# A two-layer decoder step: first weights and parameters fetched a layer ahead, semaphores cleared in two parts, page transposes spread

## What is computed

```
h  = rmsnorm(x);  x += 0.5 * rmsnorm((silu(h @ wg) * (h @ wu)) @ wd)      # f1, width 2816
h  = rmsnorm(x);  proj = h @ w_in                                          # A, B, C, gates
   A: RWKV-7 time mixing;  B: dilated window attention (8 K/V heads)
   C: latent attention: scores = q_lat . ckv + q_rope . krope over 2048 paged rows and the own ones
m  = sum_b gate_b * (y_b @ w_branch_b);  x += rmsnorm(m @ w_out)
h  = rmsnorm(x);  x += 0.5 * rmsnorm((silu(h @ wg) * (h @ wu)) @ wd)      # f2
```

## Time and profile before

| | us |
|---|---|
| median of 3 runs (3042.34 to 3046.57) | 3046.08 |
| the profiled execution | 3031.76 |
| its span | 3030.2 |
| TensorE busy | 2807.8 (93%) |
| VectorE busy | 959.1 (32%) |
| ScalarE busy | 520.8 (17%) |
| mean granted TensorE clock | 0.976 |
| first matmul of layer 0 | at 35.11 |
| first matmul of layer 1 | at 1543.98 |

### The profile page before, as it was taken

How to read it: one execution, slowest core, us unless ns; L and a number is a source line. 1 busy time by engine, 2 the same in 40 slices (tenths; PEclk the granted TensorE clock), 3 DMA queues, 4 the chain that set the end, 5 groups by cost and what they waited for, 6 DMA issues and landing times.

```text
span 3030.2 us, 44033 instructions
## 1 busy us (share of the span) xinstructions
PE 2807.8 (93%) x18588; PEld 1892.8 (62%) x18588; DVE 959.1 (32%) x2503; ACT 520.8 (17%) x1094; POOL 62.9 (2%) x84
## 2 busy tenths in 40 slices
PE   5999999999999888999869999899998998899996
PEld 3776656656656555676647676566566665567764
DVE  1220344345524342221112204444455244422211
ACT  1000121123411221100010001211334112120000
POOL 0000000000000100000000000000000001000000
PEclk9999999999999999999979999999999999999998
DMA  5434599853931423343243345998548314243431
GB/s 174 136 94 116 177 335 324 306 205 140 358 148 56 156 91 129 101 131 96 58 147 111 110 121 182 337 323 306 178 192 338 115 57 163 83 139 111 125 101 56
DMA packets 257499, 502.03 MB, mean 166 GB/s; under 512 B 10192, under 2 KB 196944, under 8 KB 242064
## 3 DMA queue, kind: packets, MB, share of 16 engines
q1 hardware_dynamic: 248848, 327.69, 32.8%
q0 software_dynamic: 8448, 171.45, 15.4%
HBM read 491.95 MB, written 140.85 MB: 209 GB/s over the span
## 4 chain that ended last, share of the span: by engine, by line
PE 89%; DVE 4%; ACT 3%; DMA 2%; issue 1%; SPq 1%; POOL 0%; DVEq 0%; ACTq 0%; POOLq 0%
PE ps L605 82%; PE ps L608 7%; DMA ring<-in_f_wu_dram 1%; DVE ring L2102 1%; DMA ring<-in_cache_mla_ckv_dram,pidx 0%; ACT big L1461 0%; ACT reg L1461 0%; DMA big<-in_cache_swa_k_dram 0%; DVE ring L2064 0%; DMA ptab<-in_page_table_dram 0%; DVE reg L1598 0%; ACT ring L1520 0%; DVE x L1609 0%; DVE ring L1992 0%; SPq L544 0%
## 5 line engine op out<-in xcount | busy, mean ns | idle before, releaser
L605 PE MATMUL ps<-h,ring 128*128 128x320 f32 (+1 forms) x3840 | 1078.2, 438 | 84.1 <-DMA ring<-in_f_wu_dram 74.0
L605 PEld LDWEIGHTS ps<-h,ring 128*128 128x128 f32 (+1 forms) x3840 | 725.4, 191 | 391.6 <-issue 99.9
L605 PE MATMUL ps<-big,ring 128*128 128x320 f32 (+3 forms) x2624 | 508.2, 371 | 22.1 <-DVE big L1621 8.1
L605 PEld LDWEIGHTS ps<-big,ring 128*128 128x128 f32 (+2 forms) x2624 | 351.4, 170 | 191.4 <-issue 41.0
L605 PE MATMUL ps<-ring,h 128*128 128x512 f32 (+3 forms) x896 | 246.2, 469 | 0.0
L1616 DVE TENSOR_TENSOR big<-ps,reg 128x320 f32<-128x320 f32 x88 | 43.2, 491 | 598.5 <-PE ps L605 598.5
L608 PE MATMUL ps<-cst,big 128*128 128x128 f32 x944 | 140.2, 284 | 26.2 <-ACT big L1461 7.3
L605 PEld LDWEIGHTS ps<-ring,h 128*128 128x128 f32 (+1 forms) x896 | 103.2, 163 | 80.6 <-issue 65.0
L1334 ACT ACTIVATE reg<-big 128x320 f32<-128x320 f32 x88 | 41.5, 471 | 647.7 <-DVE big L1616 647.7
L605 PE MATMUL ps<-reg 128*16 128x8 f32 (+13 forms) x1864 | 142.1, 276 | 2.3 <-DVE sml L1871 1.2
L1591 DVE TENSOR_TENSOR h<-h 128x320 f32<-128x320 f32 x36 | 17.7, 492 | 387.6 <-ACT h L1325 387.6
(11 more groups left out here) (255 smaller groups left out, 2196.9 us busy)
## 6 DMA issues: line engine op xcount, KB each, us to landing
out_o_swa_k_s_dram<-in_cache_swa_k_dram POOLq DMA_DIRECT2D x16, 4080.0 KB, 15.2
out_o_swa_v_s_dram<-in_cache_swa_v_dram POOLq DMA_DIRECT2D x16, 4080.0 KB, 16.4
ring<-in_w_in_dram SPq DMA_DIRECT2D x30, 2048.0 KB, 11.2
ring<-in_f_wg_dram SPq DMA_DIRECT2D x44, 1024.0 KB, 5.4
ring<-in_f_wu_dram SPq DMA_DIRECT2D x44, 1024.0 KB, 7.9
ring<-in_f_wd_dram SPq DMA_DIRECT2D x32, 1408.0 KB, 7.0
big<-in_cache_swa_k_dram SPq DMA_DIRECT2D x32, 1024.0 KB, 8.3
ring<-in_cache_swa_v_dram SPq DMA_DIRECT2D x32, 1024.0 KB, 6.9
```

The costliest lines, as they stand in the source:

```text
L605: return pe.matmul(out, lhsT, rhs, start=first, stop=last, skip_group_check=True)
```

## The change

- At the start the order of loads is x, parameters, first weight unit, constants, second and third unit. The engines wait for x alone; the constants (`s_const`) and the parameters (`s_next`) have semaphores of their own. The page table is loaded from GpSimd's queue.
- Parameters are loaded to a second buffer `parn`, for the next layer while this one is in f1, and copied to `par` by VectorE at the layer's start; the scaling of the first norm reads `parn`.
- The first three `gu` units of f1 (`HEAD`) are loaded for the next layer as the last three `d` units of f2 are used; the slots are shifted by one so that they fit (`turn` starts at 1). In the last layer they are loaded too and not used.
- 125 semaphores are cleared in f2 between the units d 0 and d 1, 18 at the layer's end. Some step semaphores are merged.
- x is stored to `yT` at the end of each layer, in two halves, and that store is waited for ahead of the last clearing.
- In each FFN the loop over k takes two column tiles instead of three, and the sum of squares stands behind k = 5, not 4.
- In `ml_sample` each group of four transposes stands alone between pieces of other work; the scores are issued in three pieces and the values in two, the values of b-2 now in the first half of batch b. VectorE's and ScalarE's lists follow.
- The product of branch c is split: the prompt's 256 columns are done in and behind the last steps of `ml_sample` (`prompt_branch`, with banks from `TAIL_BANK` = (4, 5, 0, 1, 2, 3, 7, 6)), the samples' 64 columns in `mix`.

```diff
-    slot, last, before, turn = [], {}, [], 0
+    slot, last, before, turn = [], {}, [], 1
     for i, (name, _) in enumerate(units):
...
-            at = (2, 0, 1, 0, 1, 0, 1)[name[1]]
+            at = (0, 1, 0, 1, 0, 1, 0)[name[1]]
         elif name[0] == "pg":
-            at = (0, 1, 0, 1, 1, 0)[name[1]]
+            at = (1, 0, 0, 1, 1, 0)[name[1]]
         elif name[0] in ("br", "wo"):
-            at = {"a": 0, "b": 0, "c": 0, 0: 1, 1: 2}[name[1]]
+            at = {"a": 1, "b": 0, "c": 0, 0: 1, 1: 2}[name[1]]
...
-        per_layer = [s_dve, s_par, s_sml, s_out, s_state, s_wkv, s_shin, s_shout] + s_vw + s_kw + s_slot + list(S.values())
+        to_the_end = ("ffn_a", "ffn_gu", "ffn_sg", "ffn_t", "nsum", "norm_sums", "normed", "roots", "logs", "squared", "down_d",
+                      "down_y", "x")
+        cleared_early = [s_par, s_sml, s_out, s_state, s_wkv, s_shin, s_shout] + s_vw + s_kw + [S[n] for n in STEPS if n not in to_the_end]
+        cleared_last = [s_dve] + s_slot + [S[n] for n in to_the_end] + [s_out]
...
+            def first_weights(l, u):
+                i = uidx[heads[u]]
+                at = slot_of[i] * SLOT
+                for src, k, n in units[i][1]:
+                    sp.dma_start(ring[:, at:at + k * n].rearrange("p (k n) -> p k n", k=k), src(l)).then_inc(s_head[u], 16)
+                    at += k * n
+
             sp.dma_start(x, io["xT"]).then_inc(s_once, 16)
-            for i in range(8):
-                sp.dma_start(ptab[N_PAGES * i:N_PAGES * i + N_PAGES, :], io["page_table"].rearrange("b n -> n b"), allow_slow_non_contiguous=True).then_inc(s_once, 16)
-            sp.wait_ge(s_once, ONCE)
+            sp.dma_start(parn[:, :], lay(io["params"], 0).rearrange("a p n -> p (a n)")).then_inc(s_next, 16)
+            first_weights(0, 0)
+            sp.dma_start(cst[:, :], io["consts"]).then_inc(s_const, 16)
+            for u in range(1, HEAD):
+                first_weights(0, u)
             with sp.Fori(0, DEPTH) as l:
-                sp.dma_start(par[:, :], lay(io["params"], l).rearrange("a p n -> p (a n)")).then_inc(s_par, 16)
                 sp.dma_start(kvn[:, :], lay(io["c_kv_norm"], l).rearrange("a n -> (a n)").partition_broadcast(P)).then_inc(s_par, 16)
...
                 for i, (name, srcs) in enumerate(units):
+                    if name in heads:
+                        continue
+                    if name == ("f1", "d", 0):
+                        sp.wait_ge(S["pages_ready"], 1)
+                        sp.wait_ge(S["normed"], KD)
+                        sp.dma_start(parn[:, :], lay(io["params"], 1 - l).rearrange("a p n -> p (a n)")).then_inc(s_next, 16)
+                    if name == ("f2", "d", 1):
+                        sp.wait_ge(S["ffn_a"], KF + 3)
+                        sp.wait_ge(s_out, N_ROWS_OUT)
+                        sp.wait_ge(s_wkv, 16 * 4)
+                        sp.wait_ge(s_shout, 16)
+                        for s in cleared_early:
+                            sp.sem_clear(s)
...
-                sp.wait_ge(S["x_f2"], KD)
+                for u in range(HEAD):
+                    sp.wait_ge(*used(("f2", "d", KD - HEAD + u)))
+                    first_weights(1 - l, u)
+                for half in range(2):
+                    sp.wait_ge(S["x"], ADDED["f2"] + 4 * half + 4)
+                    sp.dma_start(io["yT"][:, 4 * half:4 * half + 4, :], x[:, 4 * half:4 * half + 4, :]).then_inc(s_out, 16)
                 sp.wait_ge(S["roots"], ROOTS["f2_post"])
                 sp.wait_ge(S["norm_sums"], NORMS["f2_post"])
-                sp.wait_ge(s_out, N_ROWS_OUT)
-                sp.wait_ge(s_wkv, 16 * 4)
-                sp.wait_ge(s_shout, 16)
+                sp.wait_ge(s_out, 32)
                 sp.wait_ge(s_arrive, 4 * (l + 1))
                 sp.sem_inc(s_pad, 1)
-                for s in per_layer:
+                for s in cleared_last:
                     sp.sem_clear(s)
                 sp.sem_inc(s_go, 1)
...
-                for u in range(2):
-                    pe.wait_ge(*landed((f, "gu", u)))
+                pe.wait_ge(*arrived((f, "gu", 0)))
                 for k in range(KD):
                     pe.wait_ge(S["normed"], KD * (PRES[f + "_pre"] - 1) + k + 1)
-                    for m in range(3):
...
-                    if k == 4:
+                    if k == 5:
                         pre_sum(f + "_pre")
-                for m in range(3, KF):
+                for m in range(2, KF):
                     u = (f, "gu", m // 2)
-                    pe.wait_ge(*landed(u))
-                    pe.wait_ge(S["ffn_a"], FFN0[f] + m - 2)
+                    pe.wait_ge(*arrived(u))
+                    if m >= 3:
+                        pe.wait_ge(S["ffn_a"], FFN0[f] + m - 2)
...
@@ -1143,6 +1191,21 @@
 
                 prompt(2 * H, scores, vrow, DEAL_ML, N_DEAL)
 
+            def prompt_branch(m):
+
+                if m == 0:
+                    pe.wait_ge(*landed(("br", "c")))
+                if TAIL_BANK[m] == 4:
+                    pe.wait_ge(S["lt_act"], 9 * NB // 2)
+                    pe.wait_ge(S["lt_dve"], 9 * NB // 2)
+                if TAIL_BANK[m] == 7:
+                    pe.wait_ge(S["ml_olT"], NB)
+                if TAIL_BANK[m] < 4:
+                    pe.wait_ge(S["ml_exp"], NB)
+                w = wslot(("br", "c"), 4, D_MODEL)
+                for k in range(4):
+                    mm(ps[:, TAIL_BANK[m], 0:SEQ], w[:, k, m * P:m * P + P], yc[:, k, 0:SEQ], k == 0, k == 3)
+
             def ml_sample():
                 pe.wait_ge(S["prompt_y"], 2 * H + 16)
...
+                def own_tokens(b):
+
+                    if b >= NB:
+                        return
+                    if b >= 2:
+                        pe.wait_ge(S["ml_osb"], b - 1)
...
                     if r:
                         pe.wait_ge(S["ml_own"], min(b + 2, NB))
+                        if b:
+                            pe.wait_ge(S["ml_osb"], b)
...
+                def values(b, part):
+                    if not 0 <= b < NB:
+                        return
+                    if part == 0:
+                        pe.wait_ge(S["ml_pt"], 2 * b + 2)
+                        pe.wait_ge(S["ml_own"], min(b + 2, NB))
+                        if b:
+                            pe.wait_ge(S["ml_olT"], b)
                     o = lambda r: ps[64 * r:64 * r + NS, 7, 0:KV_LORA]
-                    for u in range(8):
+                    for u in range(4 * part, 4 * part + 4):
...
+                    if part:
+                        mm(o(0), PTl, PBc[0:NS, 2, Q_LORA:Q_LORA + KV_LORA], False, True).then_inc(S["ml_pv"], 1)
 
                 def by_channel(b):
+                    if not 0 <= b < NB:
...
+                    pe.wait_ge(S["ml_pt"], min(2 * b + 4, 2 * NB))
...
-                transposes(0)
-                for n in range(2 * NB + 3):
-                    b, a = n // 2, n % 2
-                    if n + 1 < 2 * NB:
-                        transposes(n + 1)
-                    if a == 0 and b >= 2:
-                        by_channel(b - 2)
-                    if n < 2 * NB:
-                        scores(n)
-                    if 1 <= b <= NB:
-                        shares(b - 1, a)
-                        if a:
-                            values(b - 1)
+                for g in range(5):
+                    transposed(0, g)
+                for b in range(NB + 1):
+                    n = 2 * b
+                    transposed(n + 1, 0)
+                    scores(n, 0)
+                    transposed(n + 1, 1)
+                    scores(n, 1)
+                    transposed(n + 1, 2)
+                    scores(n, 2)
+                    values(b - 2, 0)
+                    transposed(n + 1, 3)
+                    values(b - 2, 1)
+                    if b == NB:
+                        prompt_branch(0)
+                    n = 2 * b + 1
+                    transposed(n + 1, 0)
+                    own_tokens(b)
+                    scores(n, 0)
+                    transposed(n + 1, 1)
+                    scores(n, 1)
+                    transposed(n + 1, 2)
+                    if b:
+                        shares(b - 1, 0)
+                    if b == NB:
+                        prompt_branch(1)
+                    transposed(n + 1, 3)
+                    scores(n, 2)
+                    if b:
+                        shares(b - 1, 1)
+                    transposed(n + 1, 4)
+                    by_channel(b - 2)
+                prompt_branch(2)
+                values(NB - 1, 0)
+                values(NB - 1, 1)
+                prompt_branch(3)
+                by_channel(NB - 1)
+                prompt_branch(4)
                 pe.wait_ge(S["ml_olT"], NB)
                 for hd in range(H):
                     r0 = 64 * (hd % 2)
                     for c in range(2):
...
+                prompt_branch(6)
 
             def mix():
```

(63 more changed lines are left out.)

188 lines of the change are left out of this document (108 added, 80 removed).

## The result

The changed kernel takes 3013.78 us in the median of 8 runs (2997.72 to 3026.44), the kernel before 3043.36 in 8 runs beside it (3029.39 to 3049.30). The ratio is 0.9905, 95% interval 0.9875 to 0.9934: faster by some 29 us, where 88 were forecast. So the two profiles differ by 18 us and the medians by 30, and part of what the profiles differ in is chance.

The account below looks back on a forecast made before the run. TensorE, busy for 2807.8 of 3030.2 us, was taken as the bound. Terms of -21.6, -21.4, -8.8 and -36 sum to -87.8, bringing the median from 3046.08 to 2958 us; range 2944 to 2990.

Parts of the forecast that it names:

- Start: Program start: x, parameters and one weight unit loaded first let TensorE begin at 13.5 us instead of 35.11, -21.6 us.
- rival C: Program start: constants or page table arrive after 27 us and stall the sum of squares, +3 to +8 us; chance 0.16.
- Between the layers: Layer boundary: early clearing and prefetched weights let TensorE start at 1522.6 instead of 1543.98 us, -21.4 us.
- Rival B: Layer boundary: the queue delays the receipt of the x store by 5 to 10 us per layer, 2972 us; chance 0.10.
- End: Program's last part: the x store in halves and shorter clearing finish at 3019.1 instead of 3027.9 us, -8.8 us.
- Latent attention: Samples' latent attention: reordered transposes and the split product of branch c remove waits, -18 us a layer, -36 in all.
- TensorE's own work in one ... Sum 15.9, so 2.9 us of each period are waits: Samples' attention, each 18.86 us period: 15.9 us work and 2.9 us waits, of which 2.3 us would be gained.
- The tail: Up to the output projection: moving the prompt's share of branch c into gaps removes idle time and lower clock, -3.7 us.
- Rival A: Samples' attention: VectorE's order keeps TensorE waiting at the emptied bank, only 4 us a layer left, 2986 us; chance 0.15.
- Rival D: Samples' attention: page buffers come free later, so late page fetches make the kernel slower than before; chance 0.02.
- What costs nothing: FFN loops with two tiles, new slots for weight units and two more parameter copies were claimed to add no time.
- the ring places: Weight units' slots: only the second projection's column unit 2 waits longer, covered by 24 narrow matmuls and a wait, 0 us.

Follow-up runs that it names:

- e12: The changed kernel with the constants issued only when the first unit of weights has landed: 3010.8 us, 0.9873 of the kernel before.
- e2: The kernel before with only the new order of the samples' latent attention and the split product of branch c: 3035.7 us, ratio 0.9990.
- e3: The changed kernel with the weight units' ring slots as in the kernel before, the output projection's two exchanged: 2989.9 us, ratio 0.9848.
- e15: The kernel before with only the changed kernel's slots for the weight units: 3056.7 us, 1.0048 of the kernel before.
- e13: The kernel before with GpSimd's window cache copies moving 64 KB each instead of 4080 KB: 3033.2 us, ratio 0.9968.

## Why the prediction was wrong

**Start (-21.6, measured -18.2).** The mechanism was right, the term was mis-sized: 3386 KB took 15.9 us from the first issue, slower than both rates that I had as bounds, and e12 shows that only 0.6 us of it is the competing load. Why these bytes go at 213 KB a us when the weights before went at 260 isn't settled. The next needs were covered as said: constants, page table and unit 1 brought no wait, and the sum of squares follows without one, so rival C's stall did not come.

**Between the layers (-21.4, measured -21.7).** Right in each step: from the last addition (1501.94) to TensorE 9.6 us in place of 31.3. Rival B's late receipt did not come either.

**End (-8.8, measured -3.8).** The store lands 2.7 us after the last addition, as forecast, and the clearing is short. But what stood beside the store before stands alone now. SyncE's last waits, changed kernel first:

```profile
SPq L258 <- PEq L258: 7.1, 1, 7.1
SPq L587 <- DMA out_yT_dram<-x: 2.6, 1, 2.6
```

```profile
SPq L253 <- DMA out_yT_dram<-x: 4.2, 1, 4.2
SPq L253 <- PEq L253: 2.0, 1, 2.0
```

The engines' way out of the loop and to the program's end takes about 7 us after SyncE lets them go. Before, SyncE stood 4.2 us for the store and then only 2.0 for the engines, so some 4 us of their way out ran beside the store. I had costed the store and not what it covered.

**Latent attention (-36, measured -6.5 by the profile, -3 by e2, between -7 and +1).** The failed step is "TensorE's own work in one ... Sum 15.9, so 2.9 us of each period are waits". By the windows the work was 16.7 and the waits 2.2. The new order took 1.65 us of waits away, as intended, and put 0.8 us of changes in: a gain of 0.84 where 2.3 was forecast. The price of a change was never a term. It could be read: 8 transposes in a run pass in 0.93 us in the earlier trace rows, and I priced single groups by that row. (Ten changes at 0.15 would make 1.5, not 0.8; that the rest hid in the waits before is an argument, not shown.) The tail was forecast at -3.7 and lost time instead. A layer gained 3.3 us in all and its 6.4 periods 5.4, so the tail lost 2; read off the windows it lost 3.4 (47.5 us from 1113.4 to the output projection, 44.1 from 1127.8 before). In it stand 1.72 us for a result that stood behind VectorE's maximum, 2.2 us ahead of the output projection where VectorE's eight tiles of 1.04 us are the bound, and part of the time at 1.2 GHz behind both (a granted clock of 0.89 from 1113.4 to 1144.9 us, where 1.00 was forecast). The projection's own 1.7 and 3.0 us come on top. Rival A named the right place and nearly the right size, for another reason: not the bank, which was empty in time, but the changes. Rival D did not come: TensorE waits for pages twice, 2.1 us in all, and 2.3 before.

**"What costs nothing": the ring places (0, measured +15 to +17).** This step failed outright. The text saw that unit 2 would wait for unit 0, and named 24 narrow matmuls and TensorE's wait for VectorE as its cover. From its issue at 398.22 the cover is 20.1 us; it takes 22.7 to land beside GpSimd's copies, where 11.2 is the median of all such units, and I never looked up the DMA share of that part (0.95 between 435 and 460 us of the kernel before). Two layers, 2.6 us each plus time at 1.2 GHz, are not all of it: the issue waits grew too. Unit 2 was also not the only exception: by `weight_slots` the gate units 2 and 3 and the second unit of the output projection have another predecessor as well. TensorE has no wait for them.

With the measured terms the sum is -18.2 - 21.7 - 3.8 - 6.5 + 4.7 + 16 = -29.5; the medians say -29.6. The 16 for the places is from the ratios of e3 and e15, the rest from the profiles. The 28.6 us between the two profiles are more, and luck has a part in it on both sides. In the kernel before, the profiled execution lost next to nothing to the copies: its stretches of 584.3 and 580.6 us are as short as those of e13 without them, and it lies 11.6 us below its median. In the changed kernel 8.2 us of issue waits fell into layer 1, whose stretch is 598.7; e12, with the same places, had 586.7 there. With 28.6 in place of 16 the sum is -16.9, and the spans differ by -18.5. The range's upper end, 2990, was wrong because none of its terms had the other sign: the bound of the latent attention was -16, and nothing stood for the places. It was also added wrongly: 3046 - 61 with the 8 and the 4 that the text names is 2997.

## What to carry to other kernels

A weight's place in a ring is part of its schedule: a unit that loses one use of lead time must be priced by its landing beside whatever else is on the DMA engines there, not by its median over the program. And on TensorE, spreading short transposes between matmuls cost 0.15 us a change here; it pays only where the wait it removes is larger, and groups of two, with both banks in use, gave the same cover for six changes fewer. A single profile can lie 12 us from its kernel's median, so a difference between two profiles is split into terms with that in mind. When a store or a load is taken off the end of a program, look at what ran beside it.
